# A mixer chain moved wholly into the dots, the routing into the sums, and shorter groups of picks, in a two-block network on one Trainium2 core

## What is computed

```python
mod = silu(c) @ ada_w[l] + ada_b[l]                 # 6 vectors: shift, scale, gate, twice
h = modulate(x, sh1, sc1)
mix = hybrid_mixer(h, ...)                          # latent attention, short convolution, stick-breaking, @ w_o
x = layer_norm(ALPHA * x + (1 + g1) * mix, ...)
h = modulate(x, sh2, sc2)
x = layer_norm(ALPHA * x + (1 + g2) * peer(h, ...), ...)

def peer(h):                                        # 8 heads, 16 picks each: 128 picks a token
    s1, s2 = (h @ wq) against 128 keys each
    v1, i1 = top_k(s1, 16); v2, i2 = top_k(s2, 16)
    top_s, pos = top_k(all 256 sums of v1 and v2, 16)
    experts = i1 * 128 + i2 at pos
    act = gelu(dot(u_tab[experts], h))              # one row of 4 KB a pick and token
    return sum(softmax(top_s) * act * v_tab[experts])
```

## Time and profile before

| | us |
|---|---|
| median of 3 runs | 3018.24 |
| lowest and highest of them | 3010.39, 3019.68 |
| the profiled execution | 2997.13 |
| its span | 2995.3 |

### The profile page before, as it was taken

One profiled execution on the slowest core, in us unless ns is written; L12 is line 12 of the kernel. 1 busy time (PEld: TensorE's weight loads), 2 busy tenths in 40 slices (PEclk: granted clock), 3 DMA queues, 4 the chain that ended last, 5 costly groups with the idle time before them and its releaser, 6 DMA issues.

```text
span 2995.3 us, 23021 instructions
## 1 busy us (share of the span) xinstructions
PE 1797.1 (60%) x7921; PEld 1312.6 (44%) x7921; DVE 1871.4 (62%) x3359; ACT 341.8 (11%) x738; POOL 1051.9 (35%) x1045
## 2 busy tenths in 40 slices
PE   7889444185352234131326077892188999987998
PEld 5668111175141124021215066641157786476873
DVE  1435999878769886989987989558944200243001
ACT  1311101121001110001101000000013100021000
POOL 1002444577356665445765445336700000000000
PEclk9979656587575567565667589895588999988999
DMA  7357999999999999698999789999960554512443
GB/s 241 109 190 261 399 397 401 332 378 357 358 400 408 406 399 402 247 339 328 397 400 402 281 314 389 370 368 401 372 225 8 189 155 146 193 43 72 153 155 112
DMA packets 361764, 860.83 MB, mean 287 GB/s; under 512 B 23720, under 2 KB 148912, under 8 KB 361520
## 3 DMA queue, kind: packets, MB, share of 16 engines
q0 software_dynamic: 148000, 537.07, 46.5%
q1 hardware_dynamic: 213648, 322.29, 31.1%
HBM read 858.23 MB, written 1.05 MB: 287 GB/s over the span
## 4 chain that ended last, share of the span: by engine, by line
PE 36%; DMA 24%; DVE 18%; issue 15%; POOL 4%; ACT 2%; DVEq 0%; SPq 0%; ACTq 0%
PE bank L842 12%; DMA RING<-in_peer_v,EX 8%; PE bank L856 8%; PE bank L375 7%; DMA RING<-in_peer_u,EX 5%; DMA W<-in_ada_w 3%; DMA WORK<-in_peer_v,EX 3%; DVE ACC L1514 3%; POOL RING L951 2%; DMA W<-in_w_up 2%; PE bank L363 2%; PE bank L384 2%; POOL WORK L951 1%; DVE hrows L1529 1%; DMA WORK<-in_peer_u,EX 1%
## 5 line engine op out<-in xcount | busy, mean ns | idle before, releaser
L951 POOL DMA_INDIRECT RING<-in_peer_u,EX x343 | 323.5, 943 | 580.9 <-DVE EX L1490 300.2
L842 PE MATMUL bank<-HT,W 128*128 128x256 f32 x2112 | 476.6, 389 | 43.3 <-DMA W<-in_w_up 17.6
L842 PEld LDWEIGHTS bank<-HT,W 128*128 128x128 f32 x2112 | 411.8, 196 | 108.0 <-DMA W<-in_w_up 19.6
L951 POOL DMA_INDIRECT RING<-in_peer_v,EX x341 | 373.9, 1096 | 236.7 <-DVE hrows L1529 121.5
L1514 DVE SCALAR_TENSOR_TENSOR ACC<-RING,hrows 128x1024 bf16<-128x1024 f32 x343 | 402.9, 1217 | 48.6 <-DMA RING<-in_peer_u,EX 40.2
L363 PE MATMUL bank<-consts,XN 128*128 128x128 f32 x224 | 47.0, 390 | 469.8 <-DVE XN L1358 229.6
L407 PE MATMUL bank<-W,CACT 128*32 128x512 f32 x768 | 164.0, 957 | 268.3 <-DMA W<-in_ada_w 117.8
L375 PE MATMUL bank<-W,HT 128*128 128x256 f32 (+1 forms) x1120 | 245.9, 382 | 14.1 <-ACT HT L1003 7.3
L363 PEld LDWEIGHTS bank<-consts,XN 128*128 128x128 f32 x224 | 40.6, 207 | 475.6 <-DVE XN L1358 232.2
L1529 DVE SCALAR_TENSOR_TENSOR ACC<-RING,ACTS,ACC 128x1024 f32<-128x1024 f32 x168 | 215.4, 1282 | 46.2 <-DMA RING<-in_peer_v,EX 46.1
L1529 DVE SCALAR_TENSOR_TENSOR hrows<-RING,ACTS,hrows 128x1024 f32<-128x1024 f32 x168 | 216.2, 1287 | 43.0 <-DMA RING<-in_peer_v,EX 42.6
(11 more groups left out here) (323 smaller groups left out, 2259.6 us busy)
## 6 DMA issues: line engine op xcount, KB each, us to landing
W<-in_ada_w SPq DMA_DIRECT2D x48, 1024.0 KB, 13.4
W<-in_w_ada SPq DMA_DIRECT2D x48, 1024.0 KB, 14.0
W<-in_w_in SPq DMA_DIRECT2D x35, 1024.0 KB, 9.3
W<-in_w_gate SPq DMA_DIRECT2D x33, 1024.0 KB, 5.7
W<-in_w_up SPq DMA_DIRECT2D x33, 1024.0 KB, 5.5
W<-in_w_down SPq DMA_DIRECT2D x33, 1024.0 KB, 5.0
W<-in_peer_wq SPq DMA_DIRECT2D x24, 1024.0 KB, 16.7
W<-in_w_o SPq DMA_DIRECT2D x12, 1024.0 KB, 14.3
```

Source lines behind the costliest of these rows:

```text
L842: mm = pe.matmul(bs[j][:, g * S:(g + 1) * S], w[:, k, j * P:(j + 1) * P], HT[:, k, :], start=(k == 0 and g == 0), stop=(k == DC - 1 and g ...
L951: gp.indirect_dma_start(SLOT[g % NS], None, rows, bass.IndirectOffsetOnAxis(EX[:, t, k:k + 1], 0))\
```

## The change

- A round of a plan is four picks, not eight (`PER`), so there are 32 rounds in a stage, and the plans are rewritten.
- `tile1(1, t)`: all its steps up to the second normalised tile stand in the dots stage of the other tile, (t, 1-t), after picks 4, 8, 20, 28, 36, 44, 52, 56, 64, 76, 88, 92 and 96. Before, eight of them stood there (after picks 8, 16, 72 to 104, 120) and five in the sums stage.
- The routing of all four groups, 20 steps, stands in the sums stage of the other tile. Before, group 0 stood at the end of that stage and groups 1 to 3 in the tile's own dots stage. `routing` goes.
- In ScalarE's list `weigh` is split: the exponential ahead of `tile1`, the GELU (`gelu`) after `tile1` has come to the first scores (its stop moves from ahead of the attention's exponentials to there).
- The `SECOND` groups of layer 1's modulation are computed with `FIRST` in the dots of (0,0), at every fifth pick from 80; before, they were computed after the first part of `c0`.
- The `FIRST` groups of `c1`'s modulation come ahead of the second part of `c0` (its FFN), not after it.
- The context's steps are spread anew: in the sums of (0,0) after picks 4, 16, 24, 44, 60, 76, 84, 100, 120 (before 8, 8, 16, 32, 56, 72, 80, 96, 120); the FFN's eleven pairs in the dots of (1,1) 8 to 12 picks apart from pick 24; the FFN's end after pick 44 of the last sums, not 24; `c1` after 68 and 92, not 80 and 104.

```diff
--- before.py
+++ after.py
@@ -870,20 +870,19 @@
             transposes(("col", 0), "A", [CIN[:, s, :] for s in range(4)])
             block1(0)
             ada("c0", d["w_ada_2"][0], [1, 2], FIRST + SECOND + GATE1 + GATE2, beside=lambda i: gather(0, 0, 0, 6 * i + 8))
-            ada("b1", d["ada_w"][1], [0], FIRST, beside=lambda i: gather(0, 0, 0, 10 * i + 80))
+            ada("b1", d["ada_w"][1], [0], FIRST + SECOND, beside=lambda i: gather(0, 0, 0, 5 * i + 80))
             load_rows(d["b_ada_2"][0][2 * D:3 * D], d["b_ada_2"][0][5 * D:6 * D])
             load_rows(d["norm_post_mix_2"][0], d["norm_post_ffn_2"][0])
             c0 = block2("c0", 0, "c")
             next(c0)
             load_rows(d["ln2_g"][0], d["ln2_b"][0])
-            ada("b1", d["ada_w"][1], [0], SECOND)
             tile1(1, 0)
             load_rows(d["ln2_g"][0], d["ln2_b"][0])
             tile1(1, 1)
             load_rows(d["ln2_g"][1], d["ln2_b"][1])
+            ada("c1", d["w_ada_2"][1], [1, 2], FIRST)
             for _ in c0:
                 pass
-            ada("c1", d["w_ada_2"][1], [1, 2], FIRST)
             for _ in block2("c1", 1, "c", kv_only=True):
                 pass
             load_rows(d["ln2_g"][1], d["ln2_b"][1])
@@ -1158,7 +1157,6 @@
                     for hq in range(2):
                         copy((name, q, hq), dst[0:QK, 4 * hq:4 * hq + 4, :],
                              lambda b: b[0:QK, :].rearrange("p (h n) -> p h n", h=4))
-                yield
                 act.wait_ge(mark("smax", p), t + 1)
                 w = (t + 1) * P
                 for h in range(H1):
@@ -1186,12 +1184,18 @@
                     copy(("pq", q, i), PQB[:, 4 * i:4 * i + 4, :], lambda b: b[:, :].rearrange("p (u n) -> p u n", u=4))
                     for j in ((), (0,), (1,), (2, 3))[i]:
                         scores(j)
+                    if i == 1:
+                        yield
 
             def weigh(l, t):
 
                 p = f"b{l}"
                 act.wait_ge(mark("tx", p), t + 1)
                 do(A(GW[:, t, :], GW[:, t, :], ACT.Exp), mark("te", p))
+
+            def gelu(l, t):
+
+                p = f"b{l}"
                 act.wait_ge(mark("dots", p), t + 1)
                 do(A(ACTS[:, :], ACTS[:, :], ACT.Gelu), mark("gelu", p))
 
@@ -1281,25 +1285,23 @@
                 next(early)
             act.wait_ge(mark("gated", "b0"), 1)
             all_of(early)
-            all_of(ada("b1", [0], FIRST))
+            all_of(ada("b1", [0], FIRST + SECOND))
             weigh(0, 0)
+            gelu(0, 0)
             next(c0)
-            all_of(ada("b1", [0], SECOND))
-            root1("b0", 0, 5)
-            chain = tile1(1, 0)
-            next(chain)
-            weigh(0, 1)
-            all_of(chain)
-            root1("b0", 1, 6)
-            chain = tile1(1, 1)
-            next(chain)
-            weigh(1, 0)
-            all_of(chain)
+            for t in range(NT):
+                root1("b0", t, 5 + t)
+                weigh(t, 1 - t)
+                chain = tile1(1, t)
+                next(chain)
+                gelu(t, 1 - t)
+                all_of(chain)
+            all_of(ada("c1", [1, 2], FIRST))
             root1("b1", 0, 9)
+            weigh(1, 1)
             next(c0)
-            weigh(1, 1)
+            gelu(1, 1)
             all_of(c0)
-            all_of(ada("c1", [1, 2], FIRST))
             all_of(block2("c1", 1, "c", kv_only=True))
             act.wait_ge(mark("xu", "c0"), 2)
             late = ada("l1", [1], SECOND)
@@ -1501,12 +1503,13 @@
                 do(ve.tensor_tensor(w, w, PS8[:, :].unsqueeze(2).to_broadcast([P, PH, TOPK]), ALU.mult))
                 settle()
 
-            ROUNDS = PICKS // 8
+            PER = 4
+            ROUNDS = PICKS // PER
 
             def dots(p, l, t, rounds):
 
                 k0, nr = rounds
-                for k in range(8 * k0, 8 * (k0 + nr)):
+                for k in range(PER * k0, PER * (k0 + nr)):
                     g = gather(l, t, 0, k)
                     ve.wait_ge(rows_in[g % NS], 16 * (g // NS + 1))
                     if g >= 2:
@@ -1717,7 +1720,8 @@
                 yield
                 standard(p, t)
                 yield
-                yield from route(p, l, t, 0)
+                for g in range(GROUPS):
+                    yield from route(p, l, t, g)
 
             def block1(l):
                 p = f"b{l}"
@@ -1887,8 +1891,8 @@
                 def gate():
                     finish_gate(1, GA[:, 4, :], mark("gated", p))
                     yield
-                every = {k: [choices] * 3 for k in range(ROUNDS)}
-                every[7] = [choices] * 3 + [gate()]
+                every = {k: [choices] * (1 + k % 2) for k in range(ROUNDS)}
+                every[15] = [choices] * 2 + [gate()]
                 stage(l, 0, 0, every)
                 for _ in choices:
                     pass
@@ -2067,11 +2071,6 @@
                 scaled_rows(f"b{l}", t)
                 yield
 
-            def routing(l, t):
-
-                for g in range(1, GROUPS):
-                    yield from route(f"b{l}", l, t, g)
-
             def finish(*steps):
                 for s in steps:
                     for _ in s:
@@ -2079,22 +2078,17 @@
 
             c0, c1 = block2("c0", 0, "c"), block2("c1", 1, "c", kv_only=True)
             block1(0)
-            stage(0, 0, 1, {0: [c0, c0], 1: [c0], 3: [c0], 6: [c0], 8: [c0], 9: [c0], 11: [c0], 14: [c0]})
-            a = tile1(1, 0)
-            stage(0, 1, 0, {k: [a] for k in (0, 1, 8, 9, 10, 11, 12, 14)})
-            stage(0, 1, 1, {**{k: [a] for k in (0, 3, 6, 7, 8)}, 14: [a] * 3, 15: [a] * 2})
-            finish(a)
-            a, r = tile1(1, 1), routing(1, 0)
-            stage(1, 0, 0, {**{k: [r] * 2 for k in range(2, 8)}, 0: [a, r], 1: [a, r], 8: [a, r],
-                            **{k: [a] for k in (9, 10, 11, 12, 14)}})
-            finish(r)
-            stage(1, 0, 1, {**{k: [a] for k in (0, 3, 6, 7, 8)}, 14: [a] * 3, 15: [a] * 2})
-            finish(a)
-            a, r = closing(1, 0), routing(1, 1)
-            stage(1, 1, 0, {0: [a, r], 1: [c0, r], 2: [r, r], 3: [r, r], **{k: [c0, r, r] for k in range(4, 8)},
-                            8: [c0, r], **{k: [c0] for k in range(9, 15)}})
-            finish(r)
-            stage(1, 1, 1, {2: [c0], 9: [c1], 12: [c1]})
+            stage(0, 0, 1, {k: [c0] for k in (0, 3, 5, 10, 14, 18, 20, 24, 29)})
+            for t in range(NT):
+                a = tile1(1, t)
+                chain = {k: [a] for k in (0, 1, 4, 6, 8, 10, 12, 13, 15, 18, 21, 22, 23)}
+                routes = {k: [a] for k in range(3, 30) if k % 4}
+                stage(t, 1 - t, 0, chain)
+                stage(t, 1 - t, 1, routes)
+                finish(a)
+            a = closing(1, 0)
+            stage(1, 1, 0, {0: [a], 1: [c0], **{5 + (12 * i) // 5: [c0] for i in range(NF // 2)}})
+            stage(1, 1, 1, {10: [c0], 16: [c1], 22: [c1]})
             finish(c0, c1, closing(1, 1))
             for p, l in (("l0", 0), ("l1", 1)):
                 for _ in block2(p, l, "l"):
```

## The result

The changed kernel takes 3058.5 us (median of 4, 3052.2 to 3059.7); the kernel before, on the same chip, 3014.3 us (3004.4 to 3019.7). The ratio is 1.0146, 95% interval [1.0114, 1.0179]: 44 us slower, where I had forecast 42 us faster. The profiled execution took 3058.8 us, its span is 3056.8. The profiled execution of the kernel before (2997.1 us) lies 17 us under the median of its runs, so the two profiles differ by 62 us, 18 more than the medians.

The account below looks back on a forecast made before the run. Transfers were taken to bound the eight stages at 397 GB/s, VectorE second, with TensorE's last 807 us untouched. Stage forecasts summed to 1879 against 1921 us, 42 less: 2955 profiled, plus 21 to the median, 2976; range 2935 to 3015.

Parts of the forecast that it names:

- its gather waits (41 idle us before) mostly go: Sums of (0,1) and (1,0): with fewer bytes, added routing fills VectorE's idle time; 4 us of waits left, 232 us each.
- 397 GB/s: Transfer rate of the best stage, the first dots, taken as the ceiling; all stages' bytes alone then need 1790 us.
- the two full dots stages: Dots of (0,1) and (1,0), with a mixer chain in them: 230 and 232 us forecast, against 212 and 229.
- my signs of being wrong: A dots stage over 255 us, a long wait for GELU, or sums over 250 us with gather waits as before.
- Rival (b): Comes out even: gather waits of the sums stages stay, half of them kept in both; 3020 us; chance 0.14 with (d).
- (d): Order changes, but bytes freed in one stage return in the next; within 9 us of 3018; 0.14 together with Rival (b).
- So little of it adds to 223 us: Dots of (0,1) and (1,0): transfers go on filling nine slots during chain waits, so 7 us was taken, giving 230.
- at most 10: Dots of (0,0): ScalarE still copying modulation chunks when GELU is wanted; 2 us added, this the limit; stage 302 us.
- the wait of 16.7 us: VectorE's wait for ScalarE's square root, behind layer two's second modulation half; claimed to be dropped.
- the dead bins: End of sums stages: transfers near zero while GpSimd waits 24.6 and 25.9 us for the next tile's first routing; claimed to go.
- the down projection's 23.3 us: Last sums stage, (1,1): VectorE's wait for the FFN's last matmuls goes by reading after pick 44; 208 us against 235.
- Rival (c): Slower: GELU behind the chain comes late and stops everything twice; loses from 26 us lateness, 3056 at 40; chance 0.09.

Follow-up runs that it names:

- run 6: Kernel before, with all four routing groups of the next tile in the sums stages (0,1) and (1,0), none in the dots behind: ratio 1.0094.
- run 7: Kernel before, with the next tile's last chain steps and first routing group after picks 104 and 112 of two sums stages, not 120 and 128: 0.9932.
- run 5: On top of run 2: second half of layer one's modulation chunks back behind the context's first part, chain's steps spread further through the dots: 1.0056.
- run 8: run 5 with two of the four routing groups moved back into the dots stages, and ScalarE's exponential behind the mixer's first part: 0.9949.
- run 11: run 10 with one of the three routing groups of dots (1,0) and (1,1) moved into the sums stages before them: 2977.6 us, 0.989.
- run 10: Kernel before with the edits of run 7 and run 9 together: 2979.1 us, 0.9895.
- run 2: Changed kernel, with GELU ahead of the query copies on ScalarE and routing steps after picks 36 to 112 of the sums, not from 16: 1.0159.
- run 3: Changed kernel with the edits of run 1 and run 2 together: 3048 us median, 1.0163.
- run 9: Kernel before, with the context's layer-two modulation chunks ahead of its second part and the down projection read after pick 48, not 24: 0.997.
- run 12: Changed kernel, with the dots of (0,1) and (1,0) reading their second operand from SBUF, not PSUM (wrong vector, times only): span 3058.0 us against 3056.8.
- run 1: Changed kernel, with ScalarE's exponential and GELU of (0,0) after the first seven copies of layer one's modulation chunks, ahead of nine: 3052 us, 1.0178.
- run 4: run 3 with the context's eight layer-two modulation chunks back behind the FFN of layer one: 1.0134.

## Why the prediction was wrong

**The price of VectorE's work is what failed.** I moved 46.8 us of routing out of two dots stages into two sums stages and wrote that there "its gather waits (41 idle us before) mostly go". Over the three pairs of runs that differ in the place of routing groups alone or nearly so (6 and 7, 5 and 8, 11 and 10), 171 us more of VectorE's work in six sums stages made them 165 us longer, 0.97 us a us. The 174 us taken from six dots stages made these 77 us shorter, 0.44 a us. Moving 46.8 us loses 46.8 x 0.53 = 25 us, twice. The whole of it can be read without stages, from run 7 to run 6: 49 us slower, where my reading gave a gain. The rate isn't a constant: pair by pair a us cost 1.03, 0.70 and 1.26 us in the sums and gave 0.42, 0.12 and 1.10 us in the dots, and by the third pair, which moves only the first of the three groups, moving it costs nothing. In the first pair the steps of the sums also stand five at a time behind one pick, in the second one by one, so their spacing may have a part in the price.

In my sum I counted the sums stages as 237 to 232 and the dots behind at 397 GB/s whatever VectorE did. In the changed kernel the sums stages did come out as forecast (229 and 235). Of the 95 us between my 1879 and the measured 1974, 44 stand in the two full dots stages, 33 in the two stages of (0,0) and 18 in those of (1,1): the loss stands in the stages for which I had counted on 397 GB/s, and not in the sums that took the routing. That the routing is part of it is what runs 6 to 8 add. Where GELU came first and the routing later (run 2), the sums took 239 and 244 us, and dots and sums together stayed the same. Two of my signs of being wrong came, a dots stage over 255 us and a long wait for GELU; the third, sums stages over 250 us with gather waits as before, did not. Rival (b), the gather waits stay, is nearest to this mechanism; it had 0.14 of my chances, together with (d), and gave 3020.

Why a us costs one in the sums and half in the dots I can only argue. In these twelve dots stages VectorE is idle for 25 to 79 us, mostly in long waits for the chain or the FFN, which other steps can fill; in the sums for 21 to 38, in waits for rows of about 1 us each, which come back behind every step. The larger of VectorE's work and the bytes' time at 398 GB/s gave the right sign twice (runs 6 and 8) and nearly the size, and failed in the stages of run 11, where the two were within 10 us of each other.

**The rate.** I used 397 GB/s for every stage but only the first had shown it; the others had run at 347 to 388. They stayed there: 371 and 363 in the full dots stages (forecast 230 and 232 us, measured 250 and 256), 367 in (1,1) (231, measured 242). They also moved more than I had counted, 92.8 and 92.9 MB, not 88.6. With the same 708 MB, a forecast of 1879 us meant 377 GB/s on the mean; the fastest profiled execution here, one of run 7, reached 375 in 1888 us. "So little of it adds to 223 us", my step on waits, is not borne out either: the stage of (0,1), with 183 us of work, had four waits of 5.5 to 21.3 us (51 together, where I had allowed 7 us) and took 250. What each of them adds isn't shown, since no run took one away without changing something else.

**(0,0).** 302 forecast, 312 measured. VectorE's picks ended at 547 us, but the last copies of the modulation chunks came 28 us later. I took 17.4 us a chunk from the earlier trace rows and three at a time, so 5.8 us each, and priced ScalarE's lateness at 2 us, "at most 10", without summing all sixteen chunks. ScalarE's copies are one for two chunks; here are the last one ahead of the eight groups, the sixth of the eight and the eighth (start us, us):

```profile
465.52 0.60 ACT L985 ACTIVATE ROWT<-bank 128x512 f32<-128x512 f32 x1 [10.66 <-PE bank L407]
...
551.75 0.60 ACT L985 ACTIVATE ROWT<-bank 128x512 f32<-128x512 f32 x1 [12.77 <-PE bank L407]
...
571.42 0.60 ACT L985 ACTIVATE ROWT<-bank 128x512 f32<-128x512 f32 x1 [3.69 <-PE bank L407]
```

Six groups in 86.2 us are 14.4 a group, 7.2 a chunk; all eight took 106 us. They start at pick 80, from which the picks took 89 us (457.5 to 546.5). The sums stage behind it was to fall to 212 us at 397 GB/s; it stayed at 235 and 345 GB/s. Taken back (run 5), the two stages gave 33 us, of which the next took 17.

**What the parts cost.** In ratios to the kernel before, along a chain of runs that each differ from the last by one group of edits: run 11, with four small edits, 0.989; with the mixer chain inside the dots stage (run 8) 0.995; with four instead of two groups beside the sums (run 5) 1.006; with all sixteen chunks in the first dots and the steps as in the change (run 3) 1.016; the change itself 1.015. So the chain is about 18 us (with the rounds of four picks and the context's new places, which come in with it), the routing 32, the modulation chunks with the spacing of steps 32, GELU's place nothing that can be seen. Each step is uncertain by some 15 us. Against this stand the parts that were right: the wait of 16.7 us, the dead bins and the down projection's 23.3 us went. The dead bins were worth 20 us (run 7) and the down projection with the context's chunks 9 us (run 9), about half or less of their length in the trace; the wait of 16.7 us was not priced by itself.

**Rival (c)** gave 3056 at 40 us of lateness, by GELU behind the chain. The waits came (17.5 and 18.2 us) and the time came, but no run shows the one as the cause of the other: they lie below the 26 us at which I had it break even, and taking them away won nothing in run 2 (where the routing moved as well) or in run 12 (where the gathers' issues grew slower). As far as the runs show, that the time fits (c)'s 3056 is chance. From the trace of after alone I would have called it proved.

**How it should have been costed.** Per stage, VectorE's work and idle time of before stood in the earlier trace rows: sums 195.4 of 237, dots 168.8 of 212, 210.4 of 257. The dots of (1,1) have 47 us idle with VectorE at 210; to take 47 us of work from a stage that waits for FFN weights was not likely to bring it from 257 to 231. In the runs it gave 10.3 us for 45.0 of work, 0.5 for 29.5 and 16.2 for 15.6 (runs 6, 8 and 11); that the least work gave the most shows how far one profile of a stage can be off.

## What to carry to other kernels

A step moved from one stage to another is worth the difference of two prices, and the price of an engine's time must be taken in each stage by itself: here added work cost nearly its full length in the stages where the engine's only waits were short waits for data at every item, and taking work away gave on the mean less than half of it where the engine had long waits for another chain. When two resources need nearly the same time per item, a long wait in the trace may be only the place where the shortfall shows: take it away on the chip before it is called the cause. What did pay was small: to finish early the one routing group that lets the next stage's transfers start.

## What the hardware did that I had not expected

TensorE's matmuls were slowed without any wait in the trace, 35 us long in two places, and two of ScalarE's copies beside the first of them began 5.7 and 7.8 us after the one ahead of each, where in run 12 the same two followed at once. They stopped being slow when VectorE's dot products read their second operand from SBUF, not PSUM (run 12, one execution): whether by the PSUM port or because VectorE no longer ran without gaps is not separated. The profiles of the changed kernel and of runs 1 to 4 all have the slow products in both stages. It isn't proper to the change: in run 7 there were 61 us of such gaps (825 to 892 us), and some 53 to 67 in runs 6, 9, 10 and 11, but none in the profile of the kernel before, whose code there is the same; its stage lasted 215 us and theirs 207 to 225, so the gaps did not set its length. The Trainium skill, "SBUF — State Buffer", section "Who interferes with whom", says that TensorE and ScalarE never wait on anyone; for SBUF ports that may hold, but here they did go slow beside VectorE's PSUM reads.

With both operands in SBUF, GpSimd's gather issues took 1449 ns instead of 953. The same section says that a VectorE instruction with two SBUF inputs contends with a GpSimd instruction that reads SBUF; the trace agrees, by these two numbers.
